# Two transformer blocks on one core: in the first attention, the scores of query blocks 0 and 1 in one step

## The reference

```python
u = rmsnorm(h, g_mix)
z = u @ w_in                                  # queries, six key/value parts, gates, conv, merge
kc, vc = compress(kv[0], ...), compress(kv[1], ...)       # 31 compressed keys and values
# for each block of 128 queries t, each of 8 heads (2 groups of 4), dh = 64:
pc = masked_softmax(qb @ kc.T, cmp_end <= t);   o_c = pc @ vc
ps = masked_softmax(qb @ kg.T, kpos <= t);      o_s = ps @ vg    # selected blocks: all 8 are taken
pw = masked_softmax(qb @ kwb.T, window of 512); o_w = pw @ vwb
o = gates[0] * o_c + gates[1] * o_s + gates[2] * o_w
y_a = o @ w_o_nsa
```

## Time and profile before

| | |
|---|---|
| median of 3 runs | 2192.68 us (2190.61 to 2195.76) |
| profiled execution, its own time | 2187.85 us |
| its span, first to last instruction | 2186.1 us |
| mean granted clock of TensorE | 0.994 |
| TensorE busy | 2144.6 us, 98% of the span, 10162 matmuls |
| VectorE busy | 1021.7 us, 47% |
| ScalarE busy | 869.7 us, 40% |
| GpSimd busy | 932.7 us, 43% |
| chain that ended last | 89% on TensorE, 6% VectorE, 3% ScalarE |

### The profile page before, as it was taken

How to read it: one execution, slowest core, us unless ns; L and a number is a source line. 1 busy time by engine, 2 the same in 40 slices (tenths; PEclk the granted TensorE clock), 3 DMA queues, 4 the chain that set the end, 5 groups by cost and what they waited for, 6 DMA issues and landing times.

```text
span 2186.1 us, 25249 instructions
## 1 busy us (share of the span) xinstructions
PE 2144.6 (98%) x10162; PEld 1757.8 (80%) x10162; DVE 1021.7 (47%) x1643; ACT 869.7 (40%) x1358; POOL 932.7 (43%) x424
## 2 busy tenths in 40 slices
PE   9999999999999999999999999999999999999998
PEld 7877778888888887777777888888788888888886
DVE  5887775355525235566635422314653355122134
ACT  5443446344424254444434422324532244233244
POOL 5631214444444455322235444444554454444446
PEclk9999999999999999999999999999999999999999
DMA  4421112333233332211122333322223323333322
GB/s 159 146 76 49 39 49 87 96 98 104 97 96 97 97 107 77 78 49 54 48 63 87 100 97 99 98 91 86 96 87 97 97 79 97 98 97 99 99 82 85
DMA packets 53830, 193.27 MB, mean 88 GB/s; under 512 B 6097, under 2 KB 6225, under 8 KB 53713
## 3 DMA queue, kind: packets, MB, share of 16 engines
q1 hardware_dynamic: 52992, 189.81, 27.7%
q10 hardware_dynamic: 720, 1.84, 0.3%
HBM read 189.53 MB, written 2.10 MB: 88 GB/s over the span
## 4 chain that ended last, share of the span: by engine, by line
PE 89%; DVE 6%; ACT 3%; issue 1%; DMA 0%; POOL 0%; DVEq 0%; ACTq 0%; POOLq 0%
PE ps L515 27%; PE ps L517 27%; PE ps L516 27%; PE ps L699 1%; DVE ps L1171 1%; PE ps L946 1%; PE ps L679 1%; PE ps L964 1%; PE ps L691 1%; PE ps L582 1%; ACT w_hi L1820 1%; PE ps L575 1%; PE ps L971 0%; DVE xg_lo L1131 0%; PE ps L681 0%
## 5 line engine op out<-in xcount | busy, mean ns | idle before, releaser
L468 POOL TENSOR_TENSOR w_lo<-w_raw,w_hi 128x1024 fp32r<-128x1024 f32 x352 | 850.8, 2419 | 1206.4 <-ACT w_hi L1820 1206.3
L515 PE MATMUL ps<-xg_hi,w_hi 128*128 128x512 f32 x1712 | 682.9, 399 | 8.5 <-DVE xg_lo L1131 3.8
L517 PE MATMUL ps<-xg_hi,w_lo 128*128 128x512 f32 x1712 | 670.1, 391 | 0.0
L516 PE MATMUL ps<-xg_lo,w_hi 128*128 128x512 f32 x1712 | 669.6, 391 | 0.0
L1820 ACT ACTIVATE w_hi<-w_raw 128x1024 fp32r<-128x1024 f32 x352 | 372.2, 1057 | 633.2 <-PE ps L517 630.2
L515 PEld LDWEIGHTS ps<-xg_hi,w_hi 128*128 128x128 f32 x1712 | 323.2, 189 | 73.7 <-DVE xg_lo L1131 5.1
L517 PEld LDWEIGHTS ps<-xg_hi,w_lo 128*128 128x128 f32 x1712 | 322.9, 189 | 68.8
L516 PEld LDWEIGHTS ps<-xg_lo,w_hi 128*128 128x128 f32 x1712 | 323.5, 189 | 60.5
L515 PE MATMUL ps<-h_hi,w_hi 128*128 128x512 f32 x688 | 267.6, 389 | 0.0
L517 PE MATMUL ps<-h_hi,w_lo 128*128 128x512 f32 x688 | 267.6, 389 | 0.0
L516 PE MATMUL ps<-h_lo,w_hi 128*128 128x512 f32 x688 | 267.6, 389 | 0.0
(11 more groups left out here) (331 smaller groups left out, 2422.7 us busy)
## 6 DMA issues: line engine op xcount, KB each, us to landing
w_raw<-in_weights SPq DMA_DIRECT2D x352, 512.0 KB, 3.5
out_x<-mixed SPq DMA_DIRECT2D x8, 256.0 KB, 2.1
resid<-in_x SPq DMA_DIRECT2D x3, 512.0 KB, 8.2
p_raw<-in_p ACTq DMA_DIRECT2D x3, 512.0 KB, 3.6
resid<-in_x SPq DMA_DIRECT2D x2, 256.0 KB, 4.4
last_gain<-in_last_gain SPq DMA_DIRECT2D x1, 512.0 KB, 4.7
w_raw<-in_weights SPq DMA_DIRECT2D x1, 256.0 KB, 3.7
w_raw<-in_weights ACTq DMA_DIRECT2D x1, 256.0 KB, 4.0
```

The source lines that it names most:

```text
L468: pool.tensor_tensor(w_lo[:, slot, :], w_raw[:, u % RAW, :], w_hi[:, slot, :].bitcast(F32), ALU.subtract).then_inc(w_ready, 1)
L515: pe.matmul(o, w, x, start=start, stop=False)
L516: pe.matmul(o, w, xl, start=False, stop=False)
L517: return pe.matmul(o, wl, x, start=False, stop=stop)
```

## The change

Blocks 0 and 1 of a (j) have 128 and 256 keys, 384 columns together, and a bank has 512. The new offsets `S_OFF` put block 0 at column 0 and block 1 at column 128 of the head's bank; blocks 2 and 3 stay at column 0, as before. At i = 0, `head_scores` makes the products of both blocks, and one mask product for each head adds the mask to both diagonals (columns 0 to 127 and 256 to 383) from one mask that is read twice; at i = 1 there is no scores step. VectorE and ScalarE do peaks and exponentials of block 0 and then of block 1 at i = 0, ahead of the rest of that step; normalisation stays at i = 0 and i = 1. The exponentials of block 0 wait for both peaks. Apart from that, the product of the gates' unit is written to `ln_sum` instead of `T`.

```diff
+S_OFF = (0, P, 0, 0)
             def head_scores(A, s, qi, terms):
                 if s:
                     pe.wait_ge(A["exps"], 2 * s)
-                n = (qi + 1) * P
-                qs = slice(qi * P, n)
+                blocks = (0, 1) if qi == 0 else (qi,)
                 for t, (a, b) in enumerate(terms):
-                    for hd in range(2):
-                        rows = slice(hd * HD, (hd + 1) * HD)
-                        pe.matmul(ps[:, 2 + hd, 0:n], a[rows, qs], b[rows, 0:n], start=t == 0, stop=False)
+                    for q in blocks:
+                        for hd in range(2):
+                            rows = slice(hd * HD, (hd + 1) * HD)
+                            n = (q + 1) * P
+                            pe.matmul(ps[:, 2 + hd, S_OFF[q]:S_OFF[q] + n], a[rows, q * P:n], b[rows, 0:n],
+                                      start=t == 0 and q != 1, stop=False)
                 for hd in range(2):
-                    mm = pe.matmul(ps[:, 2 + hd, qs], ident_r[:], causal_r[:], start=False, stop=True)
-                mm.then_inc(A["scores"], 1)
+                    if qi == 0:
+                        o = ps[:, 2 + hd, :].rearrange("p (a b) -> p a b", b=2 * P)[:, :, 0:P]
+                        mm = pe.matmul(o, ident_r[:], causal_r[:].unsqueeze(1).to_broadcast([P, 2, P]), start=False, stop=True)
+                    else:
+                        mm = pe.matmul(ps[:, 2 + hd, qi * P:(qi + 1) * P], ident_r[:], causal_r[:], start=False, stop=True)
+                mm.then_inc(A["scores"], len(blocks))
...
-                        scores(j, i)
+                        if i != 1:
+                            scores(j, i)
...
-            scaled(U["gates"], T[:, 0:1, :])
+            scaled(U["gates"], ln_sum[:].unsqueeze(1))
...
-                        head_peaks(A1, QB * j + i, i, stat)
+                        if i != 1:
+                            head_peaks(A1, QB * j + i, i, stat)
+                        if i == 0:
+                            head_peaks(A1, QB * j + 1, 1, stat)
...
-            act.activation(ln_sum[:], T[:, 0, :], ACT.Sigmoid).then_inc(s_gate["sig"], 1)
+            act.activation(ln_sum[:], ln_sum[:], ACT.Sigmoid).then_inc(s_gate["sig"], 1)
...
             def head_exps(A, s, qi, st, probs):
-                act.wait_ge(A["peak"], s + 1)
+                act.wait_ge(A["peak"], s + 2 if qi == 0 else s + 1)
...
-                        head_exps(A1, QB * j + i, i, stat, (prob_s, prob_w)[br])
+                        if i != 1:
+                            head_exps(A1, QB * j + i, i, stat, (prob_s, prob_w)[br])
+                        if i == 0:
+                            head_exps(A1, QB * j + 1, 1, stat, (prob_s, prob_w)[br])
```

More of the change, by code:

```diff
@@ L1300, in head_peaks @@
                 dve.wait_ge(A["scores"], s + 1)
-                dve.tensor_reduce(st[:, 0, :, qi:qi + 1], ps[:, 2:4, 0:(qi + 1) * P], AX.X, ALU.max, negate=True).then_inc(A["peak"], 1)
+                dve.tensor_reduce(st[:, 0, :, qi:qi + 1], ps[:, 2:4, S_OFF[qi]:S_OFF[qi] + (qi + 1) * P], AX.X, ALU.max,
+                                  negate=True).then_inc(A["peak"], 1)
             def head_normalise(A, s, qi, st, probs, gate=None):
@@ L1960, in head_exps @@
             def head_exps(A, s, qi, st, probs):
-                act.wait_ge(A["peak"], s + 1)
+                act.wait_ge(A["peak"], s + 2 if qi == 0 else s + 1)
                 for hd in range(2):
-                    act.activation(probs[:, hd, P_OFF[qi]:P_OFF[qi] + (qi + 1) * P], ps[:, 2 + hd, 0:(qi + 1) * P], ACT.Exp,
+                    act.activation(probs[:, hd, P_OFF[qi]:P_OFF[qi] + (qi + 1) * P], ps[:, 2 + hd, S_OFF[qi]:S_OFF[qi] + (qi + 1) * P], ACT.Exp,
                                    bias=st[:, 0, hd, qi:qi + 1], accum_out=st[:, 1, hd, qi:qi + 1]).then_inc(A["exps"], 1)
```

## The result

The kernel after takes 2202.92 us, the median of 7 runs (2196.95 to 2203.58); the kernel before 2192.09 us in its 7 (2190.17 to 2195.76). The ratio is 1.0044 with a 95% interval of 1.0033 to 1.0055, so the change costs 9.6 us (7.2 to 12.1); the medians differ by 10.8. The forecast was 2196.6, which is 3.9 us more than before, with a range from 2190.5 to 2202.0. The direction and the kind of cause were right. The size was less than half of what came, and the median lies 0.9 us above the upper end of the range.

A forecast was written before the change was run, and what follows sets the result against it. TensorE, with work for 187.61 of 190 us in the attention stage, was taken as the bound. Terms −1.15 (j=0), +4.22 (odd j), +1.06 (j=4, 6) and −0.25 (j=2) gave +3.9: 2196.6 us, range 2190.5 to 2202.0.

The forecast's parts named there:

- The saving on TensorE: Scores steps of blocks 0 and 1 merged: 0.98 us saved less 0.37 added, 0.61 us for each of eight j.
- The row of equal means: Values products of 128 and 256 columns, 285 and 283 ns; from it both wider masks were taken as 0.02 us.
- the 0.2 and 1.8 us of the prediction: By the skill's table of column widths, the merge saves 0.2 us a step less and the total is 1.8 us higher.
- The waits at odd j: TensorE waits for `pt_lo` before values at j=1, 3, 5, 7; less the saving, they cost 4.22 us.
- The compressed waits: TensorE waits 1.22 us before the compressed values product at j=4 and 6; less saving and today's wait, +1.06 us.
- j = 0: First j: the step is saved, peak 1 falls in idle time, and waits before scores 3 and next j go: −1.15 us.
- Rival 2: The clock drops once more at one of three places behind compressed scores: +6.9, 2199.6 us, chance 0.22.
- The last line of the forecast: Wrong if the waits are under 0.6 us, or the stage's granted clock differs from 0.96 by more than 0.01.
- Its condition that the waits of j = 0 be gone: Right only if, among other signs, the waits of 0.45 us before scores 3 and 0.25 before next j vanish.
- Rivals 1 and 3: 1: hand-over fits under its cover, 2187.6 us, chance 0.14; 3: clock drop of j=2 goes away, 2194.4, chance 0.13.
- Rival 4: The merged mask in the scores step doesn't save: +1.8 us on top, 2198.4 us, chance 0.06.

The follow-up runs named there:

- experiment 3: a_norace with VectorE's peak of block 1 moved behind `pt_lo` and ScalarE's exponentials of block 1 behind `pt_hi`: 2185.78 us.
- experiment 4: a_norace with only ScalarE's exponentials of block 1 moved behind `pt_hi`, both peaks staying early: 2186.75 us.
- experiment 5: a_norace with ScalarE's high part of the next weight moved behind `pt_hi` at i = 0: 2190.65 us.
- a_norace: The kernel after, with ScalarE's high part of the next weight moved behind the gates' sigmoid: 2197.11 us, ratio to before 1.0021.
- experiment 6: a_norace with blocks 0 and 1 merged at odd j only, separate steps at even j: 2197.78 us, ratio to before 1.0023.
- a_late_norace2: The kernel of experiment 3, with the high parts of two weights instead of one behind the gates' sigmoid: 2186.44 us.
- b_norace: The kernel before, with ScalarE's high part of the next weight moved behind the gates' sigmoid: 2190.05 us, ratio to before 0.9986.

## Why the prediction was right in kind and short in size

- **The saving on TensorE.** Forecast 0.61 us a step, measured 0.54. The terms that were mis-sized are the two masks of 256 columns (0.07 us more than the narrow ones, not 0.02) and the added pairs (0.40, not 0.35). The row of equal means was no guide for the masks. The Trainium skill's table ("TensorE: Matmul & The Clock Gate", section "Back-to-back issue gap") has 128 cycles more for 256 columns than for 128, which is 0.11 us for two masks at 2.4 GHz. An estimate from it is that the merge saves 0.09 us a step less, 0.7 us in all; the 0.2 and 1.8 us of the prediction do not follow from it. That would have given 0.52 us, no further from the measured 0.54 than the row's 0.61.
- **The waits at odd j.** Forecast 1.52, 1.98, 1.67, 1.49; by the starts 1.47, 2.23, 1.72, 1.72. These 0.5 us more, with the smaller saving, make most of the +5.2 that stands for +4.2. The mechanism of the waits is shown by experiments 3 to 5: each time the block ahead of `pt_hi` was shortened by some 0.9 us, the wait went down by 0.92 to 0.94.
- **The compressed waits.** Forecast 1.22 us at j = 4 and 6. In the profile of after both ran at the low clock, which hides the wait but costs more; where the clock was up or back in time it shows, 1.16 us in a_norace and 1.20 and 1.18 in the second execution of after. The term was right, its condition (full clock) did not hold. In that profile the two places cost +5.45 us instead of +1.06.
- **j = 0.** Forecast −1.15, measured +1.50 in the profile. The low clock lasted from about 127 to 140 us instead of 129 to 136, and under it TensorE came too late to the waits before scores(0, 3) and scores(1, 0): they are gone from the matmuls (0.39 us is left at a weight load). The mechanism of this term was wrong: I had VectorE's peak of block 2 arrive in time once peak 1 was done early. It does not, since VectorE has work without a gap up to it, and in a_norace TensorE waits 1.44 us. That this pair still shows −0.9 us is the clock's: its low stretch at the start was about half as long (about 127 to 130 us against 129 to 135).
- **What was missed.** The start of the stage: I had taken the 1.85 us of idle time ahead of it as fixed, and read `vc_lo` with its 0.27 us from one execution. In that execution it had won its race; a shared resource whose winner changes from run to run cannot be read from one trace. Its price is 2.2 us in the wait, and taking it away gave 2.7 us in before and 4.7 in after between the means.
- **The rivals.** Rival 2, one fall more of the clock, is at work: the profile shows three falls at the later places for one before, and the mean clock is 0.9901 for 0.9923. It was given 0.22 and one fall; two came in that trace. How much of this is the merge's own is less clear: with the race away both kernels show two falls of three, and the difference of the mean clocks is worth 2.6 us with a standard error of about 1. The last line of the forecast, that it is wrong where the stage's clock differs from 0.96 by over 0.01, has come true: the clock there was 0.91 and 0.94. Its condition that the waits of j = 0 be gone was not met either where the clock was up. Rivals 1 and 3 (no waits; the fall of j = 2 gone) are out: the waits are there, and so is that fall in both profiles of after. In a_norace the place at j = 2 did stay up, with the wait that rival 3 put there, but two others fell. Rival 4 would have had the step save 0.39 us; it saves 0.54.

In sum, with the race away, the merge costs 4.9 us at full clock for 3.9 forecast; eight times the missing 0.07 of the saving make 0.6 of the difference. That the sum comes so near is in part luck: the j = 0 term was wrong in kind, and where a place ran at the low clock its wait was hidden. On top come 2.6 us of lower clock in that pair, 7.5 in all between the means. The other 2.1 us of the 9.6 are the difference of what the two kernels lose while the race is in them; that they are all its own is not shown.

Open is why after seems to lose the race more often. Both traces of after show it lost and one of two of before, which is too few to tell; six of its seven runs lie between 2202.05 and 2203.58 and one at 2196.95, the place of a_norace, which is the pattern of a race lost six times in seven, but the runs without a trace do not show it. Open is also what decides a fall of the clock. In the stage it came behind compressed scores, with their wait of 0.52 us and 24 narrow products, but not each time, and once behind a wait of 1.87 us at j = 3 (experiment 6); kernels that differ only in their order differ in how often.

## What to carry to other kernels

Two small steps of the bound engine merged into one save there part of the cost of one, here 0.54 of 0.98 us. But look at what the helper engines do for the second part: it moves ahead of everything that they do for the next hand-over, and where that hand-over has less cover than the added block, each merge costs more than it saves. Put behind the hand-over, the second part's helpers made the merged kernel no slower than the unmerged one at full clock; the new waits for them used up the saving here. To find what a change did where the clock moves, set mean time beside mean granted clock: the one tells waits and work, the other how much of the rest is the clock's.

## What the runs showed of the hardware that was not expected

A VectorE subtraction of 128 x 32 from two buffers took 1.48 us while GpSimd ran its own (2.4 us each), and 0.19 us while it was idle. Timelines of a_norace and of a_late_norace2:

```profile
122.55 2.36 POOL L469 TENSOR_TENSOR w_lo<-w_raw,w_hi 128x1024 fp32r<-128x1024 f32 x1 [2.35 <-ACT w_hi L1833]
...
123.49 1.47 DVE L1122 TENSOR_TENSOR kc_lo<-kc_f,kc_hi 128x32 fp32r<-128x32 f32 x1 [0.49 <-ACT vc_hi L1822]
...
124.88 0.28 DVE L1122 TENSOR_TENSOR vc_lo<-vc_f,vc_hi 62x128 fp32r<-62x128 f32 x1
```

```profile
124.78 0.19 DVE L1122 TENSOR_TENSOR kc_lo<-kc_f,kc_hi 128x32 fp32r<-128x32 f32 x1 [0.49 <-ACT vc_hi L1822]
124.89 0.28 DVE L1122 TENSOR_TENSOR vc_lo<-vc_f,vc_hi 62x128 fp32r<-62x128 f32 x1
```

In the first, `kc_lo` ends at 124.96, as GpSimd's instruction does (124.91): it waits for it to the end. Where a second `w_lo` is ready at that moment, `vc_lo` took 0.27 us in one execution and 2.47 in another of the same kernel; what decides it is not shown. The Trainium skill says that a VectorE instruction with two SBUF inputs contends with a GpSimd instruction that reads SBUF, over a port pair that it calls "an exclusive lock" ("SBUF — State Buffer", section "Who interferes with whom"). The traces agree, with 1.47 against 0.19 us.

The time varied by more than the race explains: the 11 runs of b_norace, where it is away, still lie between 2186.6 and 2192.4 us. And where waits were taken away, the time fell by more than they were worth: 11.2 us between the means in experiment 3, 9.6 in experiment 4 and 6.9 in experiment 5, of which 4.5, 4.6 and 4.6 at full clock. The rest goes with a higher mean clock (0.9947, 0.9939 and 0.9926 against 0.9917); whether and how the waits bring that about is not settled.
